# Two blocks of a two-stack network: projections that begin on the high parts alone, a reordered end of the delta rule, narrower waits

## The reference

```python
for i in range(DEPTH):
    x = x + 0.5 * _swiglu(_rmsnorm(x, ffn1_norm[i]), ...)
    proj = _rmsnorm(x, mix_norm[i]) @ w_in[i]
    q, k, v, z, beta_logit, alpha, hy_in = jnp.split(proj, IN_SPLITS, axis=-1)
    o_dn = _deltanet_group(q, k, v, z, beta_logit, alpha, ...)
    o_hy = _hyena_group(hy_in, ...)
    x = x + jnp.concatenate([o_dn, o_hy], axis=-1) @ w_out[i]
    x = x + 0.5 * _swiglu(_rmsnorm(x, ffn2_norm[i]), ...)
...
def step(state, inp):                       # one chunk of the delta rule
    q_i, k_i, u_i, w_i, attn_i, gl_i = inp
    v_new = u_i - jnp.einsum("bhcd,bhde->bhce", w_i, state)
    o_i = (jnp.einsum("bhcd,bhde->bhce", q_i, state)
           + jnp.einsum("bhcs,bhse->bhce", attn_i, v_new))
    ...
o = _rmsnorm(o, norm_w) * jax.nn.silu(z...)
```

## Time and profile before

| | |
|---|---|
| median of 3 runs | 2087.84 us (2087.02 to 2091.35) |
| the profiled execution, its own time | 2085.97 us |
| its span, first to last instruction | 2084.2 us |
| PE busy in it | 2026.2 us (97%) |
| DVE, ACT, POOL busy | 930.0, 1038.1, 1491.6 us (45, 50, 72%) |

### The profile page before, as it was taken

One profiled execution on the slowest core, in us unless ns is written; L12 is line 12 of the kernel. 1 busy time (PEld: TensorE's weight loads), 2 busy tenths in 40 slices (PEclk: granted clock), 3 DMA queues, 4 the chain that ended last, 5 costly groups with the idle time before them and its releaser, 6 DMA issues.

```text
span 2084.2 us, 37054 instructions
## 1 busy us (share of the span) xinstructions
PE 2026.2 (97%) x15811; PEld 1851.4 (89%) x15811; DVE 930.0 (45%) x1579; ACT 1038.1 (50%) x1543; POOL 1491.6 (72%) x652
## 2 busy tenths in 40 slices
PE   7999999999999999999999999999999999999998
PEld 7998778889989997778889988999899899999997
DVE  4550756434204450756334203655477027345750
ACT  5443436464436444446464437446544374556442
POOL 6789445458887888436358887768788877687896
PEclk9999999999999999999999999999999999999999
DMA  7656233035555655233035565545455645454653
GB/s 236 215 191 202 90 113 102 23 121 183 182 187 176 217 180 199 86 101 102 26 118 179 185 217 168 162 143 182 162 182 182 201 147 163 143 188 155 198 186 122
DMA packets 250965, 329.10 MB, mean 158 GB/s; under 512 B 9008, under 2 KB 225586, under 8 KB 250418
## 3 DMA queue, kind: packets, MB, share of 16 engines
q1 hardware_dynamic: 250802, 326.73, 47.6%
HBM read 325.66 MB, written 1.05 MB: 157 GB/s over the span
## 4 chain that ended last, share of the span: by engine, by line
PE 59%; DVE 3%; ACT 1%; issue 1%; POOL 0%; DVEq 0%; ACTq 0%
PE psA L406 12%; PE psA L408 12%; PE psA L407 12%; PE psB L407 5%; PE psB L406 5%; PE psB L408 5%; PE psB L1881 1%; PE psB L1874 1%; PE psA L2052 0%; PE psA L2054 0%; DVE small L1493 0%; PE psB L2042 0%; PE psA L1838 0%; PE psB L2195 0%; PE psA L1720 0%
## 5 line engine op out<-in xcount | busy, mean ns | idle before, releaser
L1009 POOL TENSOR_TENSOR w_lo<-raw,w_hi 128x1024 fp32r<-128x1024 f32 x600 | 1458.0, 2445 | 564.2 <-ACT w_hi L590 562.8
L406 PE MATMUL psA<-xT_hi,w_lo 128*128 128x256 f32 x3296 | 947.7, 288 | 12.2 <-DVE xT_lo L1059 7.4
L407 PE MATMUL psA<-xT_lo,w_hi 128*128 128x256 f32 x3296 | 933.2, 283 | 0.0
L408 PE MATMUL psA<-xT_hi,w_hi 128*128 128x256 f32 x3296 | 933.0, 283 | 0.0
L590 ACT ACTIVATE w_hi<-raw 128x1024 fp32r<-128x1024 f32 x600 | 630.3, 1052 | 393.6 <-PE psB L408 261.5
L406 PEld LDWEIGHTS psA<-xT_hi,w_lo 128*128 128x128 f32 x3296 | 632.7, 192 | 24.6 <-issue 20.1
L407 PEld LDWEIGHTS psA<-xT_lo,w_hi 128*128 128x128 f32 x3296 | 633.0, 192 | 3.4 <-issue 3.4
L408 PEld LDWEIGHTS psA<-xT_hi,w_hi 128*128 128x128 f32 x3296 | 632.7, 192 | 0.0
L1155 DVE TENSOR_TENSOR hT_lo<-hfull,hT_hi 128x256 fp32r<-128x256 f32 x132 | 213.7, 1650 | 2.5 <-ACT hT_hi L723 1.5
L407 PE MATMUL psB<-w_lo,hT_hi 128*128 128x512 f32 x528 | 209.6, 397 | 0.0
L406 PE MATMUL psB<-w_hi,hT_lo 128*128 128x512 f32 x528 | 208.4, 395 | 0.4 <-issue 0.4
(11 more groups left out here) (424 smaller groups left out, 2144.6 us busy)
## 6 DMA issues: line engine op xcount, KB each, us to landing
raw<-in_w_in SPq DMA_DIRECT2D x78, 1024.0 KB, 5.1
raw<-in_ffn_w_gate SPq DMA_DIRECT2D x44, 1024.0 KB, 5.2
raw<-in_ffn_w_up SPq DMA_DIRECT2D x44, 1024.0 KB, 5.2
raw<-in_ffn_w_down SPq DMA_DIRECT2D x44, 1024.0 KB, 4.8
raw<-in_w_ffn_in SPq DMA_DIRECT2D x44, 1024.0 KB, 5.0
raw<-in_w_ffn_out SPq DMA_DIRECT2D x22, 1024.0 KB, 4.7
raw<-in_w_out SPq DMA_DIRECT2D x16, 1024.0 KB, 4.8
raw<-in_w_branch_da SPq DMA_DIRECT2D x4, 1024.0 KB, 4.7
```

The costliest lines, as they stand in the source:

```text
L406: nc.tensor.matmul(o, a_lo, b_hi, start=start, stop=False, skip_group_check=skip)
L407: nc.tensor.matmul(o, a_hi, b_lo, start=False, stop=False, skip_group_check=skip)
L408: return nc.tensor.matmul(o, a_hi, b_hi, start=False, stop=stop, skip_group_check=skip)
L1009: nc.gpsimd.tensor_tensor(split_half(w_lo, n, kind), raw_half(n, kind), split_half(w_hi, n, kind).bitcast(F32), ALU.subtract)\
```

## The change

1. **Entries** (all eight). `turn_rows` writes the list `turned`: bank 0 of `psB`, bank 2 of `psA`, bank 1 of `psB`, bank 3 of `psA`. ACT and DVE read from there. That leaves banks 0 and 1 of `psA` free, and `project_entry` computes the first two halves together: 32 matmuls that need `xT_hi` alone, and then 16 with `xT_lo`. It gives both halves back at its end and waits for the low part of the second half at its start. At the program's start PE waits for `gain_kept` to be 2. The parameters' transpose of the second stack goes to bank 2 of `psB`.
2. **Waits by bank.** In `filters` the first two banks wait for `even`, the last two for `odd`; `turn_x` waits for the copy of each bank alone.
3. **Hyena.** ACT's copies of blocks 4 and 5 at i = 14 and 15; second inverse and gate at i = 19, squares at 20; `turn_back` after i = 25 and its copies on ACT at 25.
4. **End of deltanet.** v1 of a direction waits for its own part of U; DVE writes the diagonal parts first. Two thirds of o (v1 and state) are computed before v2, in place of block 6; block 6 goes behind the sums of squares, next to block 7. ACT loads the logarithm's table before the squares, and one rounding moves behind the end.

```diff
+        turned = (psB[:, 0, :], psA[:, 2, :], psB[:, 1, :], psA[:, 3, :])
...
-                    for k in {6: (0, 1), 10: (2, 3), 15: (4,), 16: (5,)}.get(i, ()):
+                    for k in {6: (0, 1), 10: (2, 3), 14: (4,), 15: (5,)}.get(i, ()):
...
-                    if i == 19:
+                    if i == 20:
                         for rb in range(RB):
                             act.wait_ge(s1["zz"].sem, s1["zz"].due(l, 2 + rb + 1))
...
-                    if i == 24:
+                    if i == 25:
                         for b in range(4):
                             if b % 2 == 0:
                                 act.wait_ge(s1["hy_back"].sem, s1["hy_back"].due(l, b // 2 + 1))
...
-                for k in range(1, 4):
+                for k in range(1, 3):
                     round_half(0, l, 94 + k + AHEAD)
 
+                A(stat[:, 45:46], eps, ACT.Ln, bias=eps)
                 for p in range(2):
                     act.wait_ge(s1["o_mm"].sem, s1["o_mm"].due(l, p + 1))
...
-                for k in range(4, 8):
+                for k in range(3, 8):
                     round_half(0, l, 94 + k + AHEAD)
...
-                    if i in (14, 18):
-                        hyena_gate(l, i // 18, 0)
-                        hyena_gate(l, i // 18, 1)
+                    if i in (14, 19):
+                        hyena_gate(l, i // 19, 0)
+                        hyena_gate(l, i // 19, 1)
...
-                for c in range(RB):
+                for c, d in ((0, 0), (1, 1), (0, 1), (1, 0)):
                     dve.wait_ge(s1["p_mm"].sem, s1["p_mm"].due(l, 26 + c + 1))
...
+                    if (c, d) != (0, 1):
+                        ins_.then_inc(s1["q_new"].sem, 1)
...
+                    pe.wait_ge(s1["spec"].sem, s1["spec"].due(l, i + 1))
                     for kc in (2 * i, 2 * i + 1):
...
             def turn_rows(st, l, q, x0):
 
+                if st == 0 and l == 0 and q == 0:
+                    pe.wait_ge(gain_kept, 2)
...
+            def project_entry(st, l, s, q):
+
+                pe.wait_ge(lo_done[st].sem, lo_done[st].due(l, s + 2))
+                for kc in range(KC):
+                    if kc % 2 == 0:
+                        pe.wait_ge(n_hi[st].sem, n_hi[st].due(l, 4 * q + kc // 2 + 1))
+                    for t in range(2):
+                        M(psA[:, t, 0:L], split_half(w_lo, s + t, "A")[:, kc, :], xT_hi[:, kc, :], start=(kc == 0), stop=False)
+                        M(psA[:, t, 0:L], split_half(w_hi, s + t, "A")[:, kc, :], xT_hi[:, kc, :], start=False, stop=False)
+                for kc in range(KC):
+                    if kc % 2 == 0:
+                        pe.wait_ge(n_lo[st].sem, n_lo[st].due(l, 4 * q + kc // 2 + 1))
+                    for t in range(2):
+                        ins_ = M(psA[:, t, 0:L], split_half(w_hi, s + t, "A")[:, kc, :], xT_lo[:, kc, :], start=False, stop=(kc == KC - 1))
+                        if kc == KC - 1:
+                            ins_.then_inc(half_used[st].sem, 1)
...
-                pe.wait_ge(s1["odd"].sem, s1["odd"].due(l, 2))
+                pe.wait_ge(s1["even"].sem, s1["even"].due(l, 2))
                 for b in range(4):
+                    if b == 2:
+                        pe.wait_ge(s1["odd"].sem, s1["odd"].due(l, 2))
...
-                pe.wait_ge(s1["spec"].sem, s1["spec"].due(l, 4))
...
-                    if i == 18:
+                    if i == 19:
                         hyena_inverse(l, 1)
                     if i == 21:
                         qk_sums(l)
-                    if i == 24:
+                    if i == 25:
                         turn_back(l)
-                    if i == 25:
                         key_products(l)
...
-                pe.wait_ge(s1["q_new"].sem, s1["q_new"].due(l, 24))
-                pe.wait_ge(s1["tu_copy"].sem, s1["tu_copy"].due(l, 24))
                 for d in range(DIRS):
+                    pe.wait_ge(s1["q_new"].sem, s1["q_new"].due(l, 23 + d))
+                    pe.wait_ge(s1["tu_copy"].sem, s1["tu_copy"].due(l, 21 + d))
```

73 lines of the change are left out of this document (40 added, 33 removed).

## The result

| | before | after |
|---|---|---|
| median, us | 2087.43 (2086.29 to 2091.35, 4 runs) | 2065.31 (2064.50 to 2065.60, 4 runs) |
| profiled execution, us | 2085.97 | 2065.15 |
| its span, us | 2084.2 | 2063.4 |

The changed kernel is faster: ratio 0.9898 with a 95% interval of 0.9882 to 0.9913, 22.1 us less by the medians and 20.8 us less by the spans. The forecast was 2068.3 us, 3.0 too high, with 2063 to 2076 as its range.

A forecast was written before the change was run, and what follows sets the result against it. PE was taken as the bound: its unchanged work plus its waits. Terms -5.1 - 0.6 + 1.2 - 2.0 - 2.3 - 1.8 - 3.3 - 5.6 = -19.5 us gave 2066.5, or 2068.3 from the median; range 2063 to 2076 us.

The forecast's parts named there:

- Ordinary entries: Five projection entries outside the mixer entries and the program's first: products start 1.03 us earlier each, -5.1 us in all.
- The rival that the row norm takes it back: Row norm or first gating, four halves after an entry, absorbs the entries' gain: +5.1, 2073.4 us; chance 10 in 100.
- Mixer entries of stack 2: Two entries gain 1.03 us each but wait 0.7 for `qkT` at the third projection: net -0.3 each, -0.6 us.
- First entry: Program start: PE's new wait for `gain_kept` delays products 1.5 us; loss 0.8 to 1.5 by the clock's rise, +1.2 taken.
- Waits for `w_lo`: After entries: refilling weight slots hides behind 5.7 us of PE's work, costing 0; such waits would show the forecast wrong.
- Waits by bank: PE's waits for the copies (1.4) and for `filt` (0.6), in two layers, go: -2.0 us.
- `hynat`: Hyena: PE's wait for ACT's copy of block 4 goes, -2.3 us in two layers.
- `Ysp`: Hyena: the two 0.9 us waits at the second inverse go, -1.8 us; two of 0.35 at the first stay.
- The rival that stack 1's projections are paced by ACT and DVE: Bank and Hyena gains are absorbed at the key products: +6.1, 2074.4 us; chance 8 in 100.
- `turn_back`: Hyena: moved one step later, removes the `zz` wait (2.0), but key products wait 2.6 in place of 1.6; counted nothing.
- End of the delta rule: Wait for U goes, -3.3 us; blocks 6 and 7 fill the `xT_lo` wait, -2.8 a layer, -5.6 us, bounds 0 and 6.2.
- POOL holds DVE up at L1373: Rival: a second POOL subtraction goes before DVE's product ahead of the key products: +4.8, 2073.1 us; chance 12 in 100.

The follow-up runs named there:

- Experiment 8: Changed kernel with key products behind projection 26, and the gains' transpose in bank 3 of psB without the wait for gain_kept: 2059.83 us, ratio to before 0.9865.
- experiment 7: Changed kernel with the gains' transpose in bank 3 of psB in place of bank 1, without PE's wait for gain_kept: 2061.75 us, ratio to before 0.9877.
- experiment 5: The changed kernel unedited, run again beside later runs: 2064.34 us, ratio to before 0.9893.
- experiment 1: Changed kernel with turn_back and its ACT copies put back one step earlier, to i = 24: 2061.59 us, ratio to before 0.9876.
- experiment 2: Changed kernel with 16 unread transposes a layer added ahead of turn_back's own, turn_back staying at i = 25: 2060.25 us, ratio to before 0.9868.
- experiment 4: Changed kernel with the key products and first turn of keys moved one half later, behind projection 26: 2061.15 us, ratio to before 0.9872.
- experiment 3: Kernel before the change, with only turn_back and its ACT copies moved to i = 25: 2089.76 us, ratio to before 1.0009.
- experiment 6: Changed kernel with DVE's product of gains at the start reading one factor from PSUM in place of SBUF: 2063.97 us, ratio to before 0.9889.
- experiment 10: Changed kernel with key products behind projection 26, gains in bank 3 of psB, and the first entry's xT_hi matmuls half by half: 2060.56 us, ratio to before 0.9867.

## Why the prediction was right, and where it wasn't

**The bound** was read rightly: PE's work stayed, and the waits listed in the earlier trace rows were the gain.

**Ordinary entries:** 1.03 us each was forecast from 639.27 - 638.24. Between the transposes and the norm's sums the entry went from 9.20 us (636.02 to 645.22) to 8.17 (630.34 to 638.51), 1.03 less. The rival that the row norm takes it back fell: no wait for it is in the list. PE's wait before the first product is 0.43 us and not 0.3, since ACT's first pair, and no longer DVE, sets it.

**Mixer entries of stack 2:** the new wait for `qkT` is 0.36 us each and not 0.7. The step that sized it was the matmuls that PE could issue meanwhile; the net gain is 0.4 each for 0.3.

**First entry:** the wait is there (2.26 us on L1674, forecast 2.2), the transposes begin at 12.81 for 12.5, the first product at 16.29 for 16.2. The loss was 0.9 us for 1.2: the rise came near 18.8 us, as before (18.7), so the lower of the two bounds (0.8) held in this execution. Experiment 8 against 7 shows that it could as well have been 1.3 more.

**Waits for `w_lo`:** the text that hides the refilling of slots behind 5.7 us of PE's work said what it would cost if that cover failed, and it named such waits among its signs of being wrong: near 100 us PE waits 1.47 us where it waited 0.61, and 0.4 in layer 2. But the term can't be told from none. The changed kernel, its second run and experiments 1, 2 and 4 are the same program up to `qk_sums` of layer 1, and they came there at 333.2 to 336.1 us, with waits for `w_lo` of 1.7 to 4.5 us over the whole trace. And experiment 3, whose entries are the old ones, has such a wait too:

```profile
99.98 0.36 PE L406 MATMUL psA<-xT_hi,w_lo 128*128 128x256 f32 x1 [1.77 <-POOL w_lo L1009]
```

So neither the late return of the first half nor the shift at the start is needed for it.

**Waits by bank, `hynat`, `Ysp`:** 7.3 us for 6.1, each 0.1 to 0.3 a layer above its row. The rows of waits were used as the whole of the gain; a wait's row leaves out that PE starts up again after it, as the first matmul of a sequence lasts longer and the next follows later (at 639.27 of the kernel before, 0.36 us long and 0.19 to the next, where 0.28 and 0.12 follow). The rival that stack 1's projections are paced by ACT and DVE fell: `qk_sums` came 3.7 us earlier a layer by these edits alone.

**`turn_back`:** here stands the step that failed, though the forecast as a whole held. "I count nothing" was right on the position of the key products (they came as late after `qk_sums` as forecast, with the wait of 2.6 that turned out 2.8), and wrong on what the wait does to the work behind it: the key products and the half after them ran at the lower clock for some 3 us in each layer. Experiments 1, 2 and 6 show the price where it fell, 1.5 us a layer.

**End of the delta rule:** the wait for U is gone, 1.75 us a layer for 1.67. Blocks 6 and 7 fill the gap before `xT_lo` wholly: 3.24 us a layer for 2.8, which is a little over the upper bound of 3.1. The wait itself cost more than its row of 2.81: from PE's last matmul before it to the first behind it were 3.21 us (429.58 to 432.79) where 0.23 is the spacing, so 3.0, and the matmul behind it came 0.1 later than usual (433.12). Another 0.1 is the wait for v2, now 0.78 for 0.88. The table load has a small share in this. The rows of the changed kernel, ACT's second square and DVE's two parts of `xT_lo`:

```profile
421.19 0.60 ACT L864 ACTIVATE osq<-psA 128x512 f32<-128x512 f32 x1 [0.30 <-PE psA L2141]
...
427.13 1.29 DVE L1459 TENSOR_TENSOR xT_lo<-oy,xT_hi 128x512 fp32r<-128x512 f32 x2
```

From the start of the square to that of `xT_lo` it is 5.94 us, where it was 6.61 (425.43 to 432.04), so the chain is only 0.7 shorter. The first part of `xT_lo` ends near 427.8 and PE comes to block 0 at 428.3, so that without those 0.7 PE would have waited some 0.2 us (an estimate from these rows).

And 3.0 us came on top: with the pauses of 1.67 and 2.81 us, the two stretches at the lower clock in layer 2 went. Nobody who reads only the list of waits sees that a pause may cost half as much again as its length; I had the granted clock in view only at the program's start.

**POOL holds DVE up at L1373** (now L1377): not by more than before. The two rows of the changed kernel:

```profile
346.46 11.60 POOL L1013 TENSOR_TENSOR w_lo<-raw,w_hi 128x1024 fp32r<-128x1024 f32 x4 [2.22 <-ACT w_hi L593]
...
350.01 3.50 DVE L1377 TENSOR_TENSOR qkvT<-qkvT,rr 128x2048 f32<-128x2048 f32 x1
```

POOL had its next subtraction ready and began four in a row, and DVE's instruction still took 3.50 us, as before (3.53). Four subtractions of 2.40 are 9.6 us; the 2.0 more are DVE's turn between two of them. So in this case DVE, which had asked first, went next.

**Two errors cancel.** The clock's -3.0 and +3.0 are of one kind, neither was in the sum, and by luck they cancel in the two profiled executions. The 3.0 us by which the forecast was high are 1.3 from the terms (20.8 for 19.5) and the rest from the step to the median: the profiled execution of before lay 1.9 below the median shown, I carried that over, and the changed kernel's profiled execution (2065.15) lies at its median. The 1.9 fit the clock as well: that execution had 0.998 where 29 have 0.9970 on average. Over all executions the lower clock takes 3 us less from the changed kernel than from the kernel before (an estimate, worked out above), so the pauses that went gave more than the merged one cost, and the forecast had no term for either.

## What to carry to other kernels

Where TensorE is the bound, don't merge two of its waits into one: two pauses of 1.0 and 1.6 us cost their length, one of 2.8 us cost 1.5 us more through the clock in 7 of 10 cases, and useless transposes put into it made the kernel faster. Before costing a moved step at nothing, ask what the idle time around it becomes in one piece, and read the granted clock in stretches of 2 to 4 us behind every long wait. A small DVE product at a place where others wait should read one factor from PSUM while GpSimd is at work (0.17 us for 1.89 here, though the whole kernel gained nothing measurable by it).

## What the runs showed of the hardware

**The clock after a pause.** Over the kernels whose traces have pauses of 2.7 us or more of PE in the mixer (before 2, after 2, experiment 3 four, experiments 5, 6 and 7 two each; ten of them at the key products), the clock went to its lower level behind 10 of 14. Behind pauses of 1.6 to 2.4 us it fell sometimes (v1 of layer 2 before, but not v1 of layer 1; the wait of 1.77 for `w_lo` in experiment 6, but not that of 1.77 in experiment 3 or those of 1.75 in experiments 7 and 8; never at the six key products that waited 1.6), in 6 of 24 cases, and twice among pauses of about 0.5 us between short matmuls of 64x64 (experiments 4 and 10). The Trainium skill (TensorE: Matmul & The Clock Gate, "Part 1: The HAM clock gate") says that when the clock first rises depends on the run, because what watches the activity isn't tied to the start of the program. Its first rise agrees: 20.96 and 22.31 us for the same beginning of a program, and in the five traces of the changed kernel's beginning PE's spacing falls to 0.12 us at 16.6 to 18.9 us. That a fall behind a pause differs from run to run too is what the 10 of 14 show.

**An "issue" idle in the inverse.** PE stands still for 0.8 to 2.4 us at one place of each layer's triangular inverse, with nothing in the profile that it waits for, in every trace of this study but in layer 2 of experiment 4, and of changing length (1.2 us in layer 2 of the changed kernel, 2.41 in the same kernel run again). With the clock's falls it makes the levels 32.1 to 36.9 us long and is as large as most terms of the sum. It has a fixed place, not in the work but in PE's instructions: counted in matmuls and weight loads from the program's start it comes before the 6462nd (6464th in the two traces of the old kernels) and before one of the 16246th to 16250th. Experiment 2 tells the two apart, since 32 instructions more a layer stand ahead there, and the count is the same, so that the pause begins 27.2 us behind the inverse's first matmul where it is 28.9 in the changed kernel:

```profile
393.03 0.27 PE L2083 MATMUL psA<-Q,TU 64*64 64x64 f32 x1 [1.79 <-issue]
```

What makes it stays open; the count shows that it goes by the number of instructions and not by what they compute.
